# Second layer's in-projections as float32r products, the out gate ahead of the heads, and a new order in the heads

## What is computed

```
h = rmsnorm(x)
xm, og, z = split(h @ w_in, 3)                 # w_in is 1024 x 6144
xc = silu(causal_conv(xm));  q, k, v = 4x4 blocks of xc, xc, xm
i, f = [q, k, v] @ w_if + b                    # gates per head and token
S = (q k^T) * decay factors;  num = S v + a (q C);  C_new = a C + (k * decay)^T v
hc = num / max(|qn|, exp(-m)) * sigmoid(og)
y = x + ((layernorm(hc) * out_g + skip * xc) * silu(z)) @ w_out
```

## Time and profile before

| | |
|---|---|
| median of 3 runs | 1197.23 us (1196.27 to 1203.04) |
| the profiled execution | 1202.19 us, its span 1200.5 us |
| PE busy | 1096.3 us, 91% of the span |
| DVE, ACT, POOL busy | 584.8, 342.2, 172.7 us |
| moved by DMA | 191.57 MB, mean 160 GB/s |
| mean granted TensorE clock | 0.956 of full speed |

### The profile page before, as it was taken

One profiled execution on the slowest core, in us unless ns is written; L12 is line 12 of the kernel. 1 busy time (PEld: TensorE's weight loads), 2 busy tenths in 40 slices (PEclk: granted clock), 3 DMA queues, 4 the chain that ended last, 5 costly groups with the idle time before them and its releaser, 6 DMA issues. The chain is left out here.

```text
span 1200.5 us, 14731 instructions
## 1 busy us (share of the span) xinstructions
PE 1096.3 (91%) x4981; PEld 716.4 (60%) x4981; DVE 584.8 (49%) x996; ACT 342.2 (29%) x641; POOL 172.7 (14%) x148
## 2 busy tenths in 40 slices
PE   5899999996896499999599999999999999996998
PEld 3677777773343277777464477446844585443776
DVE  4655555556475345553334643454444444356332
ACT  4433443423000012111244214431342224423210
POOL 5433444411000000000210102010110101010000
PEclk9999999997798699999799999999999999997999
DMA  8232222322875544444238962597239931983211
GB/s 237 71 90 75 72 69 69 87 88 88 311 241 182 183 78 143 142 141 179 62 128 298 338 161 90 203 340 238 89 134 331 285 100 42 325 317 143 70 70 72
DMA packets 140524, 191.57 MB, mean 160 GB/s; under 512 B 28482, under 2 KB 81586, under 8 KB 138902
## 3 DMA queue, kind: packets, MB, share of 16 engines
q1 hardware_dynamic: 112790, 156.25, 40.0%
q0 software_dynamic: 5808, 24.35, 6.2%
q10 hardware_dynamic: 21872, 10.28, 3.1%
HBM read 135.73 MB, written 55.24 MB: 159 GB/s over the span
## 5 line engine op out<-in xcount | busy, mean ns | idle before, releaser
L1800 DVE SCALAR_TENSOR_TENSOR state<-state,s_all,outer 128x1024 f32<-128x1024 f32 x64 | 81.3, 1283 | 103.0 <-DMA state<-in_state_C 81.2
L1989 PE MATMUL tok_ps<-w_og,hT 128*128 128x512 f32 (+1 forms) x320 | 121.5, 598 | 0.0
L1312 PE MATMUL xm_ps<-hT,shared 128*128 128x260 f32 x512 | 117.8, 389 | 1.5 <-PEq L111 1.2
L1312 PEld LDWEIGHTS xm_ps<-hT,shared 128*128 128x128 f32 x512 | 97.2, 192 | 22.2 <-issue 5.5
L625 PE MATMUL pj<-w_hi_a,h_hi_a 128*128 128x512 f32 x256 | 106.2, 415 | 3.9 <-POOL w_lo_a L450 3.9
L1660 ACT ACTIVATE outer<-v_bcast,k_cols 128x512 f32<-128x512 f32 x128 | 81.8, 710 | 85.0 <-DMA v_bcast<-keep_v_rows 84.5
L625 PE MATMUL pj<-w_lo_a,h_hi_a 128*128 128x512 f32 x256 | 101.2, 395 | 0.0
L625 PE MATMUL pj<-w_hi_a,h_lo 128*128 128x512 f32 x256 | 100.8, 394 | 0.0
L450 POOL TENSOR_TENSOR w_lo_a<-w_in,w_hi_a 128x1024 fp32r<-128x1024 f32 x32 | 77.9, 2458 | 88.7 <-ACT w_hi_a L329 49.6
L1989 PEld LDWEIGHTS tok_ps<-w_og,hT 128*128 128x128 f32 (+1 forms) x320 | 48.7, 169 | 70.1 <-issue 62.9
L1923 PE MATMUL col_ps<-hT,shared 128*128 128x260 f32 x384 | 86.7, 384 | 0.0
(11 more groups left out here) (273 smaller groups left out, 1614.4 us busy)
## 6 DMA issues: line engine op xcount, KB each, us to landing
state<-in_state_C SPq DMA_DIRECT2D x64, 512.0 KB, 5.2
out_C_sample<-state SPq DMA_DIRECT2D x64, 512.0 KB, 6.2
w_in<-in_a_w_in SPq DMA_DIRECT2D x64, 256.0 KB, 4.0
shared<-in_m_w_in SPq DMA_DIRECT2D x10, 1024.0 KB, 6.1
kv_cache<-in_cache_k SPq DMA_DIRECT2D x16, 512.0 KB, 4.8
kv_cache<-in_cache_v SPq DMA_DIRECT2D x16, 512.0 KB, 6.0
w_og<-in_m_w_in POOLq DMA_DIRECT2D x4, 2048.0 KB, 12.7
v_bcast<-keep_v_rows SPq DMA_DIRECT2D x32, 256.0 KB, 6.0
```

The source lines that it names most:

```text
L1312: last = nc.tensor.matmul(xm_ps[:, 2 * (f % 2) + s, 0:HALF], w[:, f // 2, k, (f % 2) * P:(f % 2 + 1) * P], c.hT[:, k, s * HALF:(s + 1) * H ...
L1800: nc.vector.scalar_tensor_tensor(out=state[:, k % 4], in0=state[:, k % 4], scalar=s_all[:, 0, ds(h, 1), b], in1=outer[:, g], op0=ALU.mult, ...
L1989: last = nc.tensor.matmul(tok_ps[out, u % 2, :], c.hT[:, k, t * P:t * P + p], wg[:, k, :], start=(k < sums), stop=(k >= KT - sums))
```

## The change

It does four things.

1. The norm writes its result as two float32r parts, `h_hi` (cast on ACT) and `h_lo` (the rest, on DVE), in place of `hT`.
2. The second layer's weights come by column (512 KB, rows of 512 bytes) into a ring of four. ACT casts each column, POOL makes the rest, and PE multiplies three float32r products per k-tile and half.
3. The out gate leaves the heads. After the z columns the conv stage computes 16 out gate columns in the same way; ACT applies tanh, PE transposes them, DVE copies them out of PSUM, and SP stores them to HBM. A head loads its own with POOL (1 MB and 16 KB).
4. The order of a head is rewritten on all engines, with the next head's z columns put between the values, the scores and the end, each split on POOL; `qrow`, `junk` and the tanh buffer now share memory with `sn`, `krow` and `mix`.

The core of the diff, shortened:

```diff
 class Norm: vector_store
+            need(dve, self.done, 2 * t + g - 1)
-            self.nc.vector.tensor_tensor(self.hT[:, 4 * g:4 * g + 4, t * P:t * P + p], src,
+            self.nc.vector.tensor_tensor(self.h[:, g, :, 0:p], src,
...
-                                         ALU.mult).then_inc(self.done, 1)
+                                         ALU.mult).then_inc(self.gained, 1)
+        for g in range(2):
+            dve.wait_ge(self.cast, 2 * t + g + 1)
+            self.nc.vector.tensor_tensor(lo[cols], self.h[:, g, :, 0:p], hi[cols].bitcast(F32),
+                                         ALU.subtract).then_inc(self.done, 1)
+    def scalar_cast(self, act, t):
+        for g in range(2):
+            act.wait_ge(self.gained, 2 * t + g + 1)
+            self.nc.scalar.copy(self.split[0][:, 4 * g:4 * g + 4, t * P:t * P + p],
+                                self.h[:, g, :, 0:p]).then_inc(self.cast, 1)
 build_sample_attention_and_out, ACT
-            for t in range(2, TT):
-                nm.scalar_sums(act, t)
+            nm.scalar_cast(act, 0)
+            nm.scalar_sums(act, 2)
+            nm.scalar_cast(act, 1)
+            nm.scalar_sums(act, 3)
...
 build_conv_and_gates, SP
+            def load_column(n):
+                part, h = (2, 0) if n < OG0 else (1, (n - OG0) // FH)
+                sp.wait_ge(proj, 2 * (n - FH + 1))
+                load_column_weights(sp, c, io, h, n % FH, part)
+            def store_og(f):
+                sp.wait_ge(og_taken, 2 * (f + 1))
+                sp.dma_start(io.og_keep[h, :, :, cols], og_rows[:, j, 0:NT, :]).then_inc(og_out[j], 16)
...
+            for f in range(MF):
+                if f + 25 < COLUMNS:
+                    load_column(f + 25)
+                store_og(f)
 ACT (behind the 15 DMAs)
+            def cast_w(turn, f):
+                act.wait_ge(w_in[f], 16 * (turn + 1))
+                nc.scalar.copy(w_hi[:, f], w[:, f]).then_inc(w_cast, 1)
             def head(h):
                 take(h, 0)
+                cast_w(h, FH - 1)
                 for f in range(1, FH):
                     take(h, f)
+                    cast_w(h + 1, f - 1)
                     tanh(h, f - 1)
...
+            for f in range(FH - 1):
+                cast_w(0, f)
             act.wait_ge(vec_turned, 1)
...
+            z_columns(0)
+            z_columns(1)
             act.wait_ge(gate_ready, 2)
...
+            for f in range(MF):
+                out_gate(f)
 POOL
+            with pool.Fori(0, COLUMNS // FH) as i:
+                for f in range(FH):
+                    pool.wait_ge(w_cast, FH * i + f + 1)
+                    nc.gpsimd.tensor_tensor(w_lo[:, f], w[:, f], w_hi[:, f].bitcast(F32), ALU.subtract).then_inc(w_split, 1)
 PE
+            def columns(turn, f):
+                pe.wait_ge(w_split, FH * turn + f + 1)
+                for s in range(2):
+                    cols = slice(s * HALF, (s + 1) * HALF)
+                    for k in range(KT):
+                        for n, (a, b) in enumerate(((w_hi, c.h_hi), (w_hi, c.h_lo), (w_lo, c.h_hi))):
+                            last = nc.tensor.matmul(xm_ps[:, 2 * (f % 2) + s, 0:HALF], a[:, f, k, :], b[:, k, cols],
+                                                    start=(k == 0 and n == 0), stop=(k == KT - 1 and n == 2))
+                    last.then_inc(proj, 1)
+            def turn_og(f):
+                pe.wait_ge(og_tanh, 2 * f + 2)
+                need(pe, og_taken, 2 * f)
+                for t in range(TT):
...
+                    last = nc.tensor.transpose(out, th[:, f % 2, t * P:t * P + rows(t)], c.ident[:])
+                last.then_inc(og_turned, 1)
...
+            for f in range(MF):
+                out_gate(f)
+                if f:
+                    turn_og(f - 1)
+            turn_og(MF - 1)
 build_mlstm, POOL
             def load_og(h):
-                pool.dma_start(wg[:], w_view[:, :, ds(M_WIDTH + h * M_DIM, M_DIM)]).then_inc(og_in, 16)
+                pool.dma_start(og[:, 0:NT, :], io.og_keep[ds(h, 1)].rearrange("a p t n -> (a p) t n")).then_inc(og_in, 16)
...
+                if last:
+                    pool.wait_ge(cols_done, COLS * h)
+                    load_w_y(pool, c, io)
+                else:
+                    split_z(h, 0)
                 pool.wait_ge(toks_done, TOKS * h + V + TT)
...
+                if not last:
+                    split_z(h, 1)
+                    load_z(h, 2)
+                    load_z(h, 3)
+                    split_z(h, 2)
 DVE, head
+                def columns(f):
+                    if not last:
+                        z(h, 2 * f)
+                        z(h, 2 * f + 1)
+                columns(0)
                 for t in range(NT):
                     decayed(h, t)
-                for s in range(NT):
-                    weigh(h, s)
-                sum_og(h)
-                for b in range(5):
-                    new_state(h, b)
+                new_state(h, 0)
+                weigh(h, 0)
+                weigh(h, 1)
+                new_state(h, 1)
+                weigh(h, 2)
+                weigh(h, 3)
+                new_state(h, 2)
+                columns(1)
+                new_state(h, 3)
                 norm_h(h, 0)
                 norm_h(h, 1)
-                new_state(h, 5)
+                new_state(h, 4)
...
 PE, head
-                for t in range(TT):
-                    by_token(h, V + t, 2, t)
+                for i in range(TT):
+                    by_token(h, V + i, 2, v_tile(i))
+                columns(0)
                 for t in range(NT):
                     turned_k(h, t)
-                for s in range(NT):
-                    scores(h, s)
-                out_gate(h, NT)
-                for t in range(NT):
-                    out_gate(h, t)
-                    sample_q(h, t)
...
+                sample_q(h, 0)
+                scores(h, 0)
+                scores(h, 1)
+                sample_q(h, 1)
+                scores(h, 2)
+                scores(h, 3)
+                columns(1)
+                sample_q(h, 2)
+                values(h, 0)
+                values(h, 1)
+                values(h, 2)
+                sample_q(h, 3)
+                values(h, 3)
+                prompt_state(h, 0)
+                sample_q(h, 4)
+                prompt_state(h, 1)
                 sample_q(h, 5)
+                prompt_state(h, 2)
+                sample_q(h, 6)
                 sample_q(h, 7)
+                columns(2)
                 sample_sum(h)
+                prompt_state(h, 3)
+                for t in range(TT):
+                    turned_h(h, t)
+                pe.wait_ge(toks_done, TOKS * h + NONE)
+                pe.sem_inc(toks_done, 1)
+                columns(3)
```

362 lines of the change are left out of this document (187 added, 175 removed).

## The result

The changed kernel takes 1278.5 us (median of 4 runs, 1273.8 to 1279.6) beside 1199.8 for the kernel before: a ratio of 1.065, with a 95% interval of 1.062 to 1.068. Slower was right; the size was not. The forecast was 1233 with a range up to 1256. The profiled execution took 1279.3 us (span 1277.6) where the sum had 1238.4, so 40.9 us are to be found.

The account below looks back on a forecast made before the run. It took PE's own work to set the pace. Terms -56.1 (PE work) + 4.6 + 16.8 + 2.1 + 52.2 + 16.6 gave +36.2 us: 1238.4 against the profiled execution, 1233 against the median, range 1192 to 1256.

Parts of the forecast that it names:

- A product: Second layer's columns: a float32r product of 260 columns was to take 0.1217 us, 48 of them 5.84 us a column.
- the start behind ScalarE's loads: Start of the conv stage: PE's first product waits for ACT's 15 DMAs, a cast and a POOL split, +16.8 us.
- the first update: Loop heads: the first state update on DVE was to come 23.7 us after the head's start.
- the tail from the first transposed tile: Head's end: five transposed tiles through two banks, 11.2 us, then the next head's xc load, 6.0 us.
- the last head: Last head, without z columns and xc load: 96.6 us against 80.0 by PE's work, so +16.6 us.
- the end of the stream: Heads: last state update ends 82 us (78 to 85) after the start, from 18.6 MB at 319 GB/s, 58 us.
- the loop heads' loss, 17.4: Heads: a period of 110.4 us against 93.0, so 17.4 us of new idle in each of three heads, 52.2 in all.
- the 11.2 us between stream and transposes: Heads, behind the last update: column 2 (5.84), the sample sum and the last prompt state, some 11.2 us together.
- Later splits don't bind: Conv stage: weight splits after the first don't hold PE, one each 5.84 us, four columns deep.
- The first: Rival on product price: 0.1097 us, half a float32 record; 24 us less, 1209; chance 0.22.
- the third: Rival on product price: excess twice as large where POOL splits and DVE's conv run; 27 us more, 1260; chance 0.13.
- The second: Rival on heads: states don't set them, stream ends by 74 us; four heads give back 32 us, 1201; chance 0.15.

## Why the forecast was right in sign and wrong in size

**Right.** A product (0.120 us), a column (5.85), an out gate column with its transposes in the conv stage (one every 6.32 us, 101 for sixteen where 102.1 was forecast), the start behind ScalarE's loads (16.1), the first update at +23.5, the tail from the first transposed tile (17.2), and the last head (96.3) all came within 3 us of their terms. A PE that is busy nearly all the time in the conv stage makes work there cost about its full price. Some of the agreement is luck. The conv stage was 3.1 early at its start and 6.6 late behind it. The tail's last step was to be the xc load alone, and the column at the lower clock ended at the same moment. In the last head the stream took 57.0 us, next to the 58.3 forecast from a rate that failed in the other heads.

**The whole miss.** 3.5 us are the conv stage. In the two loop heads the stream ends 6.6 and 8.9 us late, in the first head 11.9 (+107.8, where its 124.3 less the 28.4 behind the stream make 95.9). Behind the stream each of these three heads takes 3.1 to 3.6 us more than the forecast's 28.4.

**Wrong: the end of the stream.** The failing step is "From there the queues must move some 18.6 MB ... I take 82 us for the end of the last update (78 to 85)". It took the stream for a transfer with a rate, 18.6 MB at 319 GB/s. Measured over the second head's 65.1 us are 295 GB/s, some 19.2 MB. Without the stores, half of the stream's own bytes, the interval falls by only 2.2 and 8.1 us in the loop heads, with the queues 0.59 busy. With all bytes and other lists it is 60.3 or 70.1 instead of 65.1. What paces it is the loop from update to products, store and load, with each of its links in an engine's ordered list, among work that has nothing to do with the states. The same error stands at the start of the prediction, in "PE's own work sets the pace there": with 26 us of PE's work cut from a head of before, the head lost 2 to 6.

The stream of before, with other lists, took 63.1 us, and the earlier trace rows had this number. Carried over unchanged it gives 23.7 + 63.1 = 86.8 for the end, 1.8 from the measured 88.6. That would have been a better guess here, but it is no rule: the first head's interval went from 58.2 to 64.6, and the last one's from 58.8 to 57.0.

**Wrong: the first head.** It was given the loop heads' loss, 17.4, and nothing more. The change puts a cast first in ScalarE's list, and in this head alone the load behind that cast is issued after the seam. I had counted such a wait at the conv stage's start and not here. 10.1 us, shown by moving the line.

**Missized: the 11.2 us between stream and transposes.** They were 14.3 in the second head. Of the 3.1 more, 1.9 are the last sample's state products, which the term left out, and 1.2 are column 2, which TensorE ran in 7.1 us because it came out of its wait at the lower clock. Holding the clock up with filler returned nothing in the end.

**Right for a reason that was not in it: "Later splits don't bind".** PE indeed never waited for one after the first. But a split stops VectorE, and DVE went from 63.2 us busy in 110 of the conv stage to 108.6 in 120 (in part because columns also come faster). PE covered most of it, which is why the forecast for that stage came close and why an earlier start returned only a third.

**The rivals.** The first and the third fell with the 0.120 us product. The second, a stream that ends by 74, was refuted from the other side. A stream that ends later than its bytes need was no rival of mine, and the range reached up only to an end at 85.

What stays open: whether lists or transfers hold the stream once the three lists are in balance (in the interval of 60.3 us DVE still waits 12.9 us for loads and 3.7 for outer products, at a DMA share of 0.91; that order was not run without stores), and whether the 63 us of the kernel before could be shortened in the same way with the out gate left in place; that was not tried.

## What to carry to other kernels

An engine that is busy 99% of a stage may only be filling time that another chain would take anyway; before moving work out of such a stage, cut it there and look (here 26 us of work a head were worth 4). For a stream that passes through four engines' ordered lists, bytes over rate gave only a lower bound here; start from the interval that the trace shows and ask what the new order does to it. Moving one list moves the wait into the next, until all of them follow. A trace's start of a stage moves by some us from run to run, so a stage is best measured from its own start. A change with a good part and a bad part shows it by being made in halves: float32r products in the conv stage alone gave 0.991.

## What the runs showed of the hardware that I had not expected

VectorE and GpSimd stop each other. In the conv stage of the changed kernel the tap of 8 elements takes 285 ns, and 2.4 us where it starts while a split runs on GpSimd (six of sixteen do, mean 2.38 us); the tap of 512 elements takes 751 ns, and 2.8 us in that case. A third kind of tap, 128x8 with two inputs, goes from 0.22 to 2.37 us in three cases. The timelines of the two engines show one such pair, a tap started right behind a split's start and held until its end:

```profile
488.66 2.40 POOL L1262 TENSOR_TENSOR w_col_lo<-shared,w_col_hi 128x1024 fp32r<-128x1024 f32 x1 [2.68 <-ACT w_col_hi L1178]
...
488.69 2.40 DVE L1294 TENSOR_SCALAR conv_half<-st,vec 128x8 f32 x1
```

It goes the other way too: six of the 36 splits take 2.8 to 3.3 us in place of 2.4, such as the one at 451.30, which starts inside a tap of 0.75 us and takes 2.81. The Trainium skill, "SBUF — State Buffer", section "SBUF: two separate sides", says that a pair of ports shared by the two engines is an exclusive lock: a GpSimd operation, or a VectorE operation in a two-port mode or with two inputs in SBUF, gets it for the whole instruction, whichever starts first. The trace agrees with it here: 285 ns become 2.40 us beside a split of 2.40 us, and 285 again without the splits.

A float32r product has an excess of 12 and 13 ns over its columns at 2.4 GHz at the two widths seen: 0.120 us for 260 columns (0.108 at that clock) and 0.227 for 512 (0.213). The Trainium skill, "TensorE: Matmul & The Clock Gate", section "Back-to-back issue gap", gives N/2.4 + 2.5 ns as the gap of an isolated product, which would be 0.111 us for 260 columns, and some 131 ns for 512 columns in a stream with weight loads. The rows differ from both, and the rows decide.
